# Hybrid diffusion step on one core: expert rows gathered as quarter rows and turned by VectorE instead of TensorE

## The reference

```python
scores = jax.nn.sigmoid((t @ router_w).astype(jnp.float32))
sel = (scores + router_b.astype(jnp.float32)).reshape(-1, N_EXPERT_GROUPS, EXPERTS_PER_GROUP)
group_score = lax.top_k(sel, TOP_K)[0].sum(-1)
g_best = jnp.argmax(group_score, axis=-1)
sel_in = jnp.take_along_axis(sel, g_best[:, None, None], axis=1)[:, 0]
_, local = lax.top_k(sel_in, TOP_K)
ids = g_best[:, None] * EXPERTS_PER_GROUP + local
...
hid = jax.nn.silu(jnp.einsum('nd,edf->nef', t, w_gate)) * jnp.einsum('nd,edf->nef', t, w_up)
y = jnp.einsum('nef,efd->nd', hid * gates[:, :, None], w_down)
```

## Time and profile before

| | us |
|---|---|
| median of 3 timed runs (983.4 to 985.73) | 985.17 |
| the profiled execution | 980.98 |
| its span, first to last instruction | 979.2 |
| TensorE busy | 915.7 (94%) |
| VectorE busy | 493.7 (50%) |
| ScalarE busy | 181.8 (19%) |
| GpSimd busy | 161.6 (16%) |
| moved by DMA | 243.97 MB, mean 249 GB/s |

### The profile page before, as it was taken

One profiled execution on the slowest core, in us unless ns is written; L12 is line 12 of the kernel. 1 busy time (PEld: TensorE's weight loads), 2 busy tenths in 40 slices (PEclk: granted clock), 3 DMA queues, 4 the chain that ended last, 5 costly groups with the idle time before them and its releaser, 6 DMA issues.

```text
span 979.2 us, 11628 instructions
## 1 busy us (share of the span) xinstructions
PE 915.7 (94%) x4348; PEld 436.3 (45%) x4348; DVE 493.7 (50%) x1037; ACT 181.8 (19%) x386; POOL 161.6 (16%) x162
## 2 busy tenths in 40 slices
PE   3989999988899989999997999999999989999997
PEld 2423345755545545443442443433645545434432
DVE  1471574167456757333335752872446767433336
ACT  5210100266311111111112511101211111111100
POOL 4030361057400001000004200110000001000013
PEclk9999999989999989999999999999999989999999
DMA  9986945581520168999988453544250167999967
GB/s 346 396 331 261 342 185 188 162 230 51 179 113 22 44 278 322 412 420 414 421 331 299 170 209 121 222 173 172 67 225 22 44 279 268 408 423 421 421 272 300
DMA packets 71279, 243.97 MB, mean 249 GB/s; under 512 B 7617, under 2 KB 22753, under 8 KB 53809
## 3 DMA queue, kind: packets, MB, share of 16 engines
q1 hardware_dynamic: 44912, 201.12, 52.5%
q0 software_dynamic: 8528, 27.99, 7.7%
q10 hardware_dynamic: 17776, 14.04, 4.6%
HBM read 215.01 MB, written 27.33 MB: 247 GB/s over the span
## 4 chain that ended last, share of the span: by engine, by line
PE 83%; DMA 6%; DVE 5%; issue 2%; ACT 2%; POOL 1%; SPq 1%; DVEq 0%; ACTq 0%; POOLq 0%
PE bank L2278 15%; PE bank L2142 14%; PE bank L2130 14%; PE bank L2292 8%; PE bank L2111 7%; PE bank L2054 4%; PE bank L2068 4%; PE bank L2269 2%; PE bank L2181 2%; DMA ring<-in_moe_w_up 2%; DMA bz<-in_ada_w 2%; PE bank L2434 1%; DVE x_res L1437 1%; DMA ring<-in_ada_w 1%; PE bank L2581 1%
## 5 line engine op out<-in xcount | busy, mean ns | idle before, releaser
L2142 PE MATMUL bank<-ring,h_feat 128*128 128x512 f32 x320 | 145.3, 599 | 0.0
L2278 PE MATMUL bank<-ring,uv 128*32 128x512 f32 (+2 forms) x592 | 142.2, 596 | 3.1 <-ACT uv L1118 2.4
L2142 PEld LDWEIGHTS bank<-ring,h_feat 128*128 128x128 f32 x320 | 58.0, 190 | 59.8 <-issue 59.7
L2278 PEld LDWEIGHTS bank<-ring,uv 128*32 128x32 f32 (+2 forms) x592 | 45.9, 128 | 70.3 <-issue 66.0
L1683 DVE TENSOR_TENSOR uv<-uv,bank 128x256 f32<-128x256 f32 x25 | 10.5, 421 | 127.8 <-ACT uv L1126 127.8
L2292 PE MATMUL bank<-ring,uv 128*32 128x512 f32 (+2 forms) x296 | 72.7, 596 | 1.2 <-issue 0.6
L2111 PE MATMUL bank<-ring,h_feat 128*128 128x512 f32 x144 | 65.3, 609 | 2.7 <-issue 2.7
L2130 PE MATMUL bank<-ring,h_feat 128*128 128x512 f32 x144 | 64.1, 597 | 0.0
L982 POOL TENSOR_SCALAR h_tok<-h_tok 128x384 f32<-128x384 f32 (+1 forms) x40 | 44.1, 1115 | 61.4 <-DVE h_tok L1936 61.4
L1006 POOL DMA_INDIRECT uv<-h_rows,small x23 | 21.8, 948 | 193.2 <-PE bank L2269 158.3
L2278 PE MATMUL bank<-bz,uv 128*64 128x512 f32 (+1 forms) x112 | 49.4, 594 | 0.0
(11 more groups left out here) (321 smaller groups left out, 1380.1 us busy)
## 6 DMA issues: line engine op xcount, KB each, us to landing
bz<-in_ada_w SPq DMA_DIRECT2D x12, 2048.0 KB, 7.4
ring<-in_moe_w_gate SPq DMA_DIRECT2D x20, 1024.0 KB, 11.5
ring<-in_moe_w_up SPq DMA_DIRECT2D x20, 1024.0 KB, 13.5
ring<-in_moe_w_down SPq DMA_DIRECT2D x20, 1024.0 KB, 15.0
h_tok<-in_moe_w_down SPq DMA_DIRECT2D x12, 1024.0 KB, 15.4
y_rows<-uv SPq DMA_DIRECT2D x23, 512.0 KB, 14.5
ring<-in_ada_w SPq DMA_DIRECT2D x4, 2048.0 KB, 10.4
y_rows<-uv ACTq DMA_DIRECT2D x1, 6656.0 KB, 25.5
```

The costliest lines, as they stand in the source:

```text
L2142: last = mm(jbank(key)[:, :], HT[:, cc, P * t:P * (t + 1)], blk_ap(("out", layer, b))[:, cc, :], start=cc == 0, stop=cc == DC - 1)
L2278: last = mm(bank[2][32 * q:32 * (q + n), :], XT[:, b, cc, 32 * q:32 * (q + n)], w[:, :, cc, :], start=cc == 0, stop=cc == DC - 1)
```

## The change

The rows of passes 1 and up are no longer turned by TensorE. Each gather is cut into four: piece i fetches the 32 rows of quarter i, and each row as four quarter rows of 256 features (1 KB), so that partition 32g + r gets features 256g and up of row r. VectorE then turns each 32x32 block in one instruction (`turn_rows`, a STREAM_TRANSPOSE of 128x1024) straight into `XT`. ScalarE's and VectorE's copies from PSUM of these passes are gone. The rows of pass 0 still go through TensorE. `XG` becomes free when VectorE has turned it (`xt_dve`).

The index columns become columns of pieces (`piece_i`), each with 4 x token + quadrant: 16 small products for the three fixed places (before gate and up of pass 0) and 24 for the others, two more for the last pass's tokens. The late tables move out of the fifth expert buffer into `PS`, `Hr` and `HTr`, and SyncE's wait on `late_idx_mm` before place 4's load is dropped. The prompt flags come from two more products (`prompt_sums`) instead of a comparison on VectorE.

```diff
 # tables
+PIECES = (4 * FIXED, 4 * FIXED + PLACES // 32 * RANKED)
-        ov_at = [2048]
+        ov_at = [4096]
         def late(n):
             ov_at[0] += n
-            assert ov_at[0] <= 6144
-            return BZ[:, ov_at[0] - n:ov_at[0]]
+            assert ov_at[0] <= 5120
+            return HTr[:, ov_at[0] - n:ov_at[0]]
...
+        def piece_column(p, k):
+            return FIXED * k + p if p < FIXED else PIECES[0] + RANKED * k + p - FIXED
 # SyncE
                 for p in range(FIXED, WSLOTS):
                     ex = ranked_expert(p)
-                    if p == 3:
+                    if p == FIXED:
                         sp.wait_ge(logits_done, TT * (layer + 1))
                         sp.wait_ge(h2_stored, 16 * TT * (layer + 1))
-                    if p == 4:
-                        sp.wait_ge(late_idx_mm, layer + 1)
 # GpSimd
+                def gather_pieces(e):
+                    for i in range(4):
+                        at_ = piece_column(*plan.quarter(e, i))
+                        nc.gpsimd.indirect_dma_start(
+                            out=XG[:, e % 3, 256 * i:256 * i + 256], out_offset=None,
+                            in_=h2_rows[layer].rearrange("t (g f) -> (t g) f", g=4),
+                            in_offset=bass.IndirectOffsetOnAxis(ap=piece_i[:, at_:at_ + 1], axis=0))\
+                            .then_inc(gathered[e % 3], 16)
...
-                        pool.wait_ge(xt_mm, NPASS * layer + e - 2)
-                    gather(plan.tile(e), e % 3, gathered[e % 3])
+                        pool.wait_ge(xt_dve, NPASS * layer + e - 2)
+                    gather_pieces(e)
 # VectorE
+                def turn_rows(e):
+                    s = e % 3
+                    dve.wait_ge(gathered[s], 64 * (plan.gathers_before(s) + e // 3 + (s > 0)))
+                    nc.vector.transpose(XT[:, s, :, :].rearrange("p c (i b) -> p i c b", i=4),
+                                        XG[:, s, :].rearrange("p (i a c) -> p i c a", i=4, c=DC)).then_inc(xt_dve, 1)
                 def body(e, b, round_, round_before):
+                    if 1 < e < passes - 1:
+                        turn_rows(e + 1)
                     dve.wait_ge(silu_done, base + e + 1)
                     nc.vector.tensor_tensor(hid, silu_g, bank[2][:, FF:2 * FF], ALU.mult).then_inc(hid_done, 1)
                     if e == 0:
-                        pass_indices(layer, 1, 2, NPASS)
-                        read_xt(1, base + 2)
+                        turn_rows(1)
+                        piece_indices(layer, 1)
                         route_slots(layer)
-                    if 0 < e < passes - 2:
-                        read_xt((b + 1) % 3, base + e + 2)
                     if e == 1:
+                        turn_rows(2)
                         row_tables(layer)
 # TensorE
+                for k in range(PLACES // 32 if part else 4):
+                    rows = slice(0, P if k < 4 else PLACES - P)
+                    toks = (idx_low[:, 0:FIXED] if part == 0 else tok_low) if k < 4 else tok_high[rows]
+                    at_ = piece_column(FIXED if part else 0, k)
+                    for g in range(4):
+                        last = mm(piece_tokens[32 * g:32 * g + 32, at_:at_ + toks.shape[-1]],
+                                  ident[rows, 32 * (k % 4):32 * (k % 4) + 32], toks, start=True, stop=True)
...
                 def body(e, b, round_, _):
-                    pe.wait_ge(xt_act, base + e + 1)
+                    if e == 0:
+                        piece_indices(layer, 0)
+                        pe.wait_ge(xt_act, layer + 1)
                     pe.wait_ge(xt_dve, base + e + 1)
...
-                    if e < passes - 2:
-                        next_rows()
```

More of the change, by code:

```diff
@@ L145, in plan_tiles, with quarter @@
         return tiles
+    def quarter(self, e, i):
+        q, _, p, k = next(a for a in self.tiles[e] if a[0] <= i < a[0] + a[1])
+        return p, k + i - q
     def tile(self, e):
@@ L1568, in rank_experts, with piece_indices @@
                 nc.vector.tensor_reduce(tok_high[high], by_rank[high], AX, ALU.add).then_inc(ids_ready, 1)
[L1569 to L1571 removed]
+            def piece_indices(layer, part):
+                at_ = slice(PIECES[0], PIECES[1]) if part else slice(0, PIECES[0])
                 dve.wait_ge(idx_mm, (TT + 2) * layer + TT + 1 + part)
[L1574 removed]
+                if part:
+                    nc.vector.tensor_copy(last_place, last_pass_tokens)
+                nc.vector.tensor_scalar(piece_i[:, at_], piece_tokens[:, at_], 4.0, quadrant, ALU.mult, ALU.add).then_inc(idx_ready, 1)
             def route_weights(layer):
@@ L2249, in out_projection, with piece_indices @@
                 indices(TT - 1)
-            def pass_indices(layer, part, passes):
+            def piece_indices(layer, part):
                 pe.wait_ge(idx_ready, 4 * layer + 1 + part)
@@ L2254, in pass_indices @@
                     pe.wait_ge(ids_ready, 2 * (layer + 1))
-                for e in passes:
-                    tile = PLANS[layer].tile(e)
-                    for q, n, p, k in PLANS[layer].tiles[e]:
-                        out = idx_pass[32 * q:32 * (q + n), tile:tile + 1]
-                        if k < 4:
-                            toks = idx_low[:, p:p + 1] if p < FIXED else tok_low[:, p - FIXED:p - FIXED + 1]
-                            last = mm(out, ident[:, 32 * k:32 * (k + n)], toks, start=True, stop=True)
-                        else:
-                            last = mm(out, ident[0:PLACES - P, 32 * (k - 4):32 * (k - 4 + n)],
-                                      tok_high[0:PLACES - P, p - FIXED:p - FIXED + 1], start=True, stop=True)
+                for k in range(PLACES // 32 if part else 4):
[5 more added lines that the diff above has]
+                                  ident[rows, 32 * (k % 4):32 * (k % 4) + 32], toks, start=True, stop=True)
+                if part:
+                    for q, n, p, k in PLANS[layer].tiles[-1]:
+                        rows, toks = (slice(0, P), tok_low) if k < 4 else (slice(0, PLACES - P), tok_high)
+                        last = mm(last_pass_tokens[32 * q:32 * (q + n)], ident[rows, 32 * (k % 4):32 * (k % 4 + n)],
+                                  toks[rows, p - FIXED:p - FIXED + 1], start=True, stop=True)
                 last.then_inc(idx_mm, 1)
@@ L2341, in body @@
                                       stop=k == 2 * TT - 1)
+                        for k in (0, TT):
+                            last = mm(prompt_sums, late_place[:, k, :], late_tiles[:, k, :], start=k == 0, stop=k == TT)
                         last.then_inc(late_idx_mm, 1)
-                    def next_rows():
-                        nxt = (b + 1) % 3
-                        pe.wait_ge(gathered[nxt], arrivals(round_ + 1, nxt, 16))
-                        xt_transposes(nxt).then_inc(xt_mm, 1)
-                    if e < passes - 2:
-                        next_rows()
                     if 0 < e < passes - 1:
```

60 lines of the change are left out of this document (21 added, 39 removed).

## The result

| | before | changed |
|---|---|---|
| median of 6 timed runs, us | 983.93 (979.61 to 985.73) | 975.56 (973.19 to 976.96) |
| ratio, 95% interval | | 0.9924 (0.9905 to 0.9943) |
| span of the profiled execution, us | 979.2 | 971.2 |
| TensorE busy, us | 915.7 | 897.7 |
| VectorE busy, us | 493.7 | 523.0 |

I forecast 986.5 us and no change as likeliest. The kernel went the other way. That the time still lies inside the range (974 to 996 us) is no merit of the sum, since the range was drawn wide enough to take in rival B. B's number (978 us) was nearest, but not its account: B left pass 1 where it was and took 3 us off each layer, where pass 1 came 2.0 and 1.0 us later and the stages gained 6.0 and 4.9.

A forecast was written before the change was run, and what follows sets the result against it. TensorE and the DMA engines were taken to bind the expert stages together. Layer 0 +0.2, layer 1 +0.8 and DMA +0.5 gave +1.5 us on 985.17: forecast 986.5 us, own range 981 to 992, whole range 974 to 996.

The forecast's parts named there:

- rival B: Four gather pieces land nearly as fast as the whole, so pass 1 keeps its time: 978 us; chance 0.25.
- The first gather: Before pass 1 of layer 0: last piece lands at 383.3 us behind weights, pass 1 starts 8.1 us later.
- Rows 8: Queue view before the change, read as: an engine takes one packet from each queue in turn, whatever its size.
- DMA work of the cut: All passes: 23 gathers cut in four cost 3.7 us of all DMA engines, +0.5 us on the path.
- The fifth buffer: Place 4's earlier load fills the hole at 386 to 388 us, at most 1.5 us DMA time, path unchanged.
- The saving per pass: From pass 3 on, 0.95 us of TensorE transposes gone each: 9.5 us in layer 0, 8.6 in layer 1.
- Turning on VectorE: Block transpose takes 1.2 us (0.7 to 2.5), on the path in passes 1 and 2, hidden from pass 3.
- rival D: Block transpose costs 2.5 us; passes 1 and 2 per layer pay 1.3 us more each: 989 to 991; chance 0.08.
- The low clock: Gate and up of pass 1, after TensorE idles 9 us, run at clock 0.50: 2.5 us charged.
- Rival C: Gathers cannot keep up behind full weight queues, delaying passes 2 and 3, +4.5 us per layer: 995 us; chance 0.17.

The follow-up runs named there:

- e2: Changed kernel with one gather of 128 whole 4 KB rows per pass instead of four pieces; 1008.61 us, ratio 1.0282, with two overflow passes in layer 1.
- e7: Changed kernel with place 3's weights asked for only when the first gather has landed; 982.32 us, ratio 0.9995 to before.
- e6: Changed kernel with the block transpose of 128x1024 done twice for every pass from 3 on; 973.67 us, ratio 0.9897 to before.
- e5: Kernel before the change with only the late tables moved and place 4's load no longer waiting; 986.2 us, ratio 1.0031 to before.
- e1: Changed kernel with SyncE's wait for the late tables' products before place 4's load put back; 990.84 us, ratio 1.0096 to before.

## Why the prediction was wrong, point by point

**The first gather: the step that failed.** The prediction put a piece at 8 packets of 1 KB per engine and so the cut gather at "32 turns x (0.31 + 0.045) = 11.4 us". It is 4 x 2 = 8 packets of 4 KB, as many as the whole one. I expected the last piece 21.1 us after the first transposes of the stage (383.3 less 362.17); it came 14.2 after them (378.49 less 364.31), where the whole gather came at 10.3. Of the 6.9 us between, 1.2 are an earlier issue (16 index products took 0.43 us and not 1.6), and the rest is the way: the last piece took 7.36 us from issue to landing and not 13.3. What remains is latency: each piece takes 2.9 us alone and 6.4 to 7.4 behind weights, and the fourth is issued 4.0 us after the first. e2 takes the cut away, e7 the weights in flight; either alone gives 3.1 and 3.0 us back at pass 1, not their sum, because 11.3 us after pass 0 VectorE's own hidden rows and turning become the limit (1.43 us of waiting for them in e2's row). So pass 1 was late by 2.0 and 1.0 us and not by 8.1, and pass 2 by 2.7 and 1.6 (4.1 and 1.8 in the second profile) and not by 9.7 and 9.4. On a sum of +1.5 us this one term was 7 to 8 us too high in each layer.

Rows 8 had been read rightly: one packet of each queue in turn. In the changed kernel too queue 0 and queue 1 move 73 and 76 packets in 392 to 394 us; 21 and 3 of them are signals, and the counts of rows 8 held 15 signals of queue 1 each, so the counts are equal if a signal takes a turn as well. In e2 three whole gathers stood behind full weights one after another and landed at 384.68, 388.44 and 392.22 us: 3.8 us apart, the 8 x (0.31 + 0.16) of the prediction. (The shares of the window at 66.5 us give 0.32 for an 8 KB packet, not 0.31, which changes nothing.) Wrong was the step from there to "a packet is an element", for which no row of before spoke, since its elements were 4 KB, as large as a packet gets. The Trainium skill (DMA: Bandwidth & Descriptors, SWDGE vs HWDGE vs iDMA) states that a packet of a transfer issued by GpSimd is preferably at most 4096 bytes and at most 64 descriptors, and is where an engine switches; by that rule the cut costs no turns for its data, and the packet counts above agree. The rule of the Trainium skill that I weighed (same page, Queues, rings and completion order), 9 to 17 descriptors, gave rival B. Its direction was right, the count was not: a data packet here holds 4 quarter rows.

**DMA work of the cut: wrong in kind, near in size.** Forecast 3.7 us of all engines from four times as many data packets, 0.5 us on the path. Bytes and data packets stayed: 243.95 MB moved against 243.97, and the same 128 packets of 4 KB per pass; new are 48 signals per pass, 0.01 us each. But the full engines moved 413 GB/s where kernels with one gather moved 421 and 422. Taken over some 100 us per layer that is, as an estimate, 2 us of all engines in each, so about the 3.7 by luck. On the path it is part of the 1.85 us at pass 8 of layer 1, which e2 did not have. What makes the difference no run takes apart; in 35 to 115 us after layer 1's pass 0 an 8 KB packet took 0.318 us in the mean with four pieces (the changed kernel twice, e6) and 0.312 with one gather (e2, e5).

**The fifth buffer: wrong as well.** "It was hidden anyway", worth 1.5 us at most. That was read from the hole of before, at 386 to 388 us. But the late products moved from 386.3 to 392.0 us in the changed kernel. In e1, whose stage begins 1.7 us earlier, the DMA share falls to 0.54 at 380 us, while those products end only near 390. This is the hole that the wait would leave now: 7.5 us in layer 0, and it costs 15 to 18 us in both layers together. The bounds of a removed wait have to be read in the order after the change. e5 shows the other side: without TensorE's saving the early load only slows gather 2. In my sum the load was gone either way, so this error did not move the forecast; it hid what carries the gain.

**The saving per pass: right.** Layer 0 runs from pass 2 to pass 12 in 113.88 us, 122.62 before: 8.7 us less, where I had 9.5 for ten passes. Nine lose 0.97 each; the tenth, from pass 11 to 12, takes 16.03 us against 16.04, since a wait of 1.53 us for VectorE's reading of the sums of pass 10 (at 505.97) stands where the transposes were. Layer 1: 104.99 against 111.51, 6.5 us less. The 8.6 forecast lack 1.2 us at pass 8, where the wait for weights grew from 0.69 to 1.85, and 0.95 at the last pass, as in layer 0.

**Turning on VectorE: right in place, low in size.** 1.2 us taken, 2.03 measured, inside 0.7 to 2.5. It stands on the path at pass 1 alone; e6 shows that it is hidden behind the head. Of rival D (2.5 us, paid at passes 1 and 2) 0.8 us at pass 1 of each layer came true.

**The low clock: right.** A pause of 4.4 us, a granted clock of 0.50 behind it, and 1.5 us lost in the one profile, 2.8 in the other, where I had charged 2.5. In layer 1 of e2 and e7 the clock was low behind a wait of only 1.43 us (9.91 and 9.89 us for gate and up), so the length of the pause does not decide it alone; what does stays open.

**Rival C** did not come: no pass from 3 on waits for a gather.

By its own steps with the measured sizes the sum is +2.7 - 8.7 in layer 0 and +1.6 - 6.5 in layer 1, -10.9 us together, of which the span shows 8.0 and the two sets of timed runs 8.4 and 9.6.

## What to carry to other kernels

Before a transfer is priced by its packets, count the packets of a like one in the queue view, and divide its bytes by them: the unit need not be the element. Look at the GB/s at full share as well, since equal bytes in equal packets can still take longer. Where a wait is removed together with other edits, look for the idle time that it would leave in the new order, not in the old one. And where two resources are full at once, an edit that frees one is worth only what the other follows: here TensorE's saving without the early load (e1) and the early load without the saving (e5) are both slower than before, and together they are 1% faster.

## What the runs showed of the hardware

A gather issued by GpSimd packs elements of 2, 1 and 0.5 KB into packets of 4 KB, 64, 32 and 16 of them for 128 elements; at 0.25 KB it is one packet of 2 KB per engine. Alone such gathers took 4.6, 3.5, 3.0, 2.8 and 2.4 us from 4 KB down, each read as the time from its issue to the start of what waited for it, so below 1 KB nearly all is latency. Behind full weight queues a piece of two packets per engine took 6.4 us and a whole of eight 9.0: about 5.5 us fixed and 0.43 per packet, near the sum of an 8 KB and a 4 KB packet (0.31 + 0.16). The block transpose of 128x1024 float32, read and written with strides, took 2.03 us against 1.23 for an addition of that size. With the DMA engines full, kernels that cut each gather in four moved 413 GB/s and kernels with one gather 421 and 422 in the same window, though a gather has as many data packets either way. And one kernel's stage can differ from itself by 1.4 us behind a pause of TensorE: gate and up took 8.62 us in one profile and 9.91 in the other, where the granted clock was still 0.50 in 380 to 382 us, 3 us after they had begun.
